# The down products of an expert's second token tile move to the gate and up banks of PSUM

## What is computed

```python
def expert_block(args):
    xb, e = args
    hdn = jax.nn.silu(xb @ w_gate[e]) * (xb @ w_up[e])
    return hdn @ w_down[e]
...
y = y_buf[dest] * gate_sorted[:, None].astype(x.dtype)
return jnp.zeros_like(xf).at[tok_sorted].add(y).reshape(b, s, d)
```

## Time and profile before

| what | value |
|---|---|
| median of 3 runs | 1715.93 us (1715.03 to 1716.71) |
| the profiled execution | 1715.41 us |
| its span, first to last instruction | 1713.2 us |
| its mean granted TensorE clock | 0.973 of full speed |
| TensorE matmuls busy | 1615.4 us, 94% |
| VectorE busy | 1086.8 us, 63% |
| ScalarE busy | 659.3 us, 38% |
| start of expert 1, start of expert 15 | 1053.77 us, 1641.83 us |
| from one expert's start to the next, experts 2 to 15 | 41.63 to 41.68 us |

### The profile page before, as it was taken

How to read it: one execution, slowest core, us unless ns; L and a number is a source line. 1 busy time by engine, 2 the same in 40 slices (tenths; PEclk the granted TensorE clock), 3 DMA queues, 4 the chain that set the end, 5 groups by cost and what they waited for, 6 DMA issues and landing times. The chain is left out here.

```text
span 1713.2 us, 25162 instructions
## 1 busy us (share of the span) xinstructions
PE 1615.4 (94%) x9494; PEld 1398.8 (82%) x9494; DVE 1086.8 (63%) x1799; ACT 659.3 (38%) x919; POOL 340.6 (20%) x271
## 2 busy tenths in 40 slices
PE   6999999999999999999999289999999999999993
PEld 4888888888888888888887178999999999999982
DVE  3436867557676468665586756555676667666676
ACT  2324424143332343342432324344555445544540
POOL 1100005100052001250000012222332323232332
PEclk8999999999999999999999679999999999999997
DMA  7332245332434225352223626666777777777761
GB/s 232 127 99 74 100 146 198 99 98 87 160 139 158 74 75 186 108 182 92 80 93 123 258 84 200 190 203 204 235 250 249 228 238 251 252 228 239 249 182 56
DMA packets 118922, 279.46 MB, mean 163 GB/s; under 512 B 14689, under 2 KB 16865, under 8 KB 118289
## 3 DMA queue, kind: packets, MB, share of 16 engines
q1 hardware_dynamic: 92112, 190.78, 32.8%
q0 software_dynamic: 26112, 84.95, 16.8%
q10 hardware_dynamic: 576, 2.10, 0.3%
HBM read 232.80 MB, written 48.40 MB: 164 GB/s over the span
## 5 line engine op out<-in xcount | busy, mean ns | idle before, releaser
L1054 PE MATMUL mix_acc<-mix_xT_high,mix_w_high 128*128 128x512 f32 x640 | 256.4, 401 | 7.5 <-DVE mix_w_low L791 7.5
L791 DVE TENSOR_TENSOR mix_w_low<-mix_w_raw,mix_w_high 128x2048 fp32r<-128x2048 f32 x73 | 168.5, 2309 | 144.7 <-ACT mix_w_high L646 144.4
L1056 PE MATMUL mix_acc<-mix_xT_high,mix_w_low 128*128 128x512 f32 x640 | 250.9, 392 | 0.0
L1055 PE MATMUL mix_acc<-mix_xT_low,mix_w_high 128*128 128x512 f32 x640 | 250.1, 391 | 0.0
L646 ACT ACTIVATE mix_w_high<-mix_w_raw 128x2048 fp32r<-128x2048 f32 x73 | 139.8, 1915 | 243.4 <-PE mix_acc L1056 224.2
L1789 DVE TENSOR_TENSOR moe_gate_up_low<-kept_w_gate_up_raw,moe_gate_up_high 128x2048 fp32r<-128x2048 f32 x64 | 146.6, 2291 | 80.3 <-ACT moe_gate_up_high L1661 80.3
L2117 PE MATMUL moe_gate_psum<-moe_xT_high,moe_gate_up_high 128*128 128x288 f32 x512 | 154.2, 301 | 1.4 <-DVE moe_xT_low L1806 1.4
L2119 PE MATMUL moe_up_psum<-moe_xT_high,moe_gate_up_low 128*128 128x288 f32 x512 | 152.1, 297 | 0.0
L2118 PE MATMUL moe_gate_psum<-moe_xT_low,moe_gate_up_high 128*128 128x288 f32 x512 | 151.9, 297 | 0.0
L2118 PE MATMUL moe_up_psum<-moe_xT_low,moe_gate_up_high 128*128 128x288 f32 x512 | 151.8, 296 | 0.0
L2117 PE MATMUL moe_up_psum<-moe_xT_high,moe_gate_up_high 128*128 128x288 f32 x512 | 151.6, 296 | 0.0
(11 more groups left out here) (441 smaller groups left out, 3493.2 us busy)
## 6 DMA issues: line engine op xcount, KB each, us to landing
mix_w_raw<-in_w_in SPq DMA_DIRECT2D x57, 1024.0 KB, 5.3
kept_w_gate_up_raw<-in_w_gate SPq DMA_DIRECT2D x32, 1024.0 KB
kept_w_gate_up_raw<-in_w_up SPq DMA_DIRECT2D x32, 1024.0 KB
kept_w_down_raw<-in_w_down SPq DMA_DIRECT2D x32, 1024.0 KB, 10.1
mix_w_raw<-in_w_out SPq DMA_DIRECT2D x16, 1024.0 KB, 5.0
mix_x_rows<-in_x POOLq DMA_DIRECT2D x16, 512.0 KB, 4.5
kept_conv_or_residual<-in_x POOLq DMA_DIRECT2D x16, 512.0 KB, 5.8
x<-kept_conv_or_residual POOLq DMA_DIRECT2D x12, 512.0 KB, 3.3
```

Source lines behind the costliest of these rows:

```text
L791: dve.tensor_tensor(wl[:, stage % 2], raw[:, stage % 2], wh[:, stage % 2].bitcast(F32), ALU.subtract).then_inc(split_l, 1)
L1054: pe.matmul(out, ah, bh, start=first, stop=False)
L1055: pe.matmul(out, ah, bl, start=False, stop=False)
L1056: return pe.matmul(out, al, bh, start=False, stop=last)
```

## The change

The down products of tile B go to `pg[1]` and `pu[1]`, the banks of the gate and up products of chunks 1 and 3. All that reads them there is redirected. The wait of `down` for B on the copies of A is gone, in expert 15 too the wait on A's sum. `down` for A now waits for the copies of the previous expert's A alone. `gate_up` for chunk 1, the next writer of bank 1, waits for the copies of the previous expert's B.

```diff
--- before.py
+++ after.py
@@ -1466,6 +1466,8 @@
         pg = [ps(f"gate_psum{k}", [P, BANK]) for k in range(2)]
         pu = [ps(f"up_psum{k}", [P, BANK]) for k in range(2)]
         py = [ps(f"y_psum{k}", [P, BANK]) for k in range(2)]
+
+        pb = (pg[1], pu[1])
         px = [ps(f"xT_psum{k}", [P, BANK]) for k in range(2)]
 
         xT_at = (px, (pg[0], pu[0]), px[0:1])
@@ -1698,7 +1700,7 @@
                 act.wait_ge((a_used, b_used)[k], r * NE + e + 1)
                 if e:
                     act.wait_ge(added, r * (LAST * COLS * 16) + e * (COLS * 16))
-                act.activation(Y[:, k, 0:BANK], py[0][:], ACT.Copy,
+                act.activation(Y[:, k, 0:BANK], (py, pb)[k][0][:], ACT.Copy,
                                scale=gate[:, COLS * e + k:COLS * e + k + 1]).then_inc(y_act, 1)
 
             def y_quarters(r, e):
@@ -1822,7 +1824,7 @@
                 dve.wait_ge((a_used, b_used)[k], r * NE + e + 1)
                 if e:
                     dve.wait_ge(added, r * (LAST * COLS * 16) + e * (COLS * 16))
-                dve.tensor_scalar(Y[:, k, BANK:], py[1][:], gate[:, COLS * e + k:COLS * e + k + 1], None, ALU.mult)\
+                dve.tensor_scalar(Y[:, k, BANK:], (py, pb)[k][1][:], gate[:, COLS * e + k:COLS * e + k + 1], None, ALU.mult)\
                    .then_inc(y_dve, 1)
 
             def one_hots(r):
@@ -2016,7 +2018,7 @@
                     parts = ((rows, px[1][:, 0:DQ], last[:, 1, LAST:]),)
                 else:
                     c = COLS * LAST + k
-                    parts = [(rows[:, q * BANK:(q + 1) * BANK], py[q][:], gate[:, c:c + 1]) for q in range(2)]
+                    parts = [(rows[:, q * BANK:(q + 1) * BANK], (py, pb)[k][q][:], gate[:, c:c + 1]) for q in range(2)]
                 for part, ps_part, scale in parts:
                     ins = dve.scalar_tensor_tensor(out=part, in0=ps_part, scalar=scale, in1=part,
                                                    op0=ALU.mult, op1=ALU.add)
@@ -2145,6 +2147,9 @@
                 elif n >= 2:
                     pe.wait_ge(hid_done, r * (NE * FC) + n - 1)
                 pe.wait_ge(gu_l, r * (NE * FC) + n + 1)
+                if f == 1 and e:
+                    for done in (y_act, y_dve):
+                        pe.wait_ge(done, r * (2 * LAST) + 2 * e)
                 for c in range(KC):
                     for k, out in enumerate((pg, pu)):
                         ins = three(out[f % 2][:, 0:CAP], wh[:, n % RING, c, k], wl[:, n % RING, c, k],
@@ -2152,15 +2157,9 @@
                 ins.then_inc(gu_used, 1)
 
             def down(r, e, k):
-                if k == B:
-                    if e < LAST:
-                        for done in (y_act, y_dve):
-                            pe.wait_ge(done, r * (2 * LAST) + 2 * e + 1)
-                    else:
-                        pe.wait_ge(end_sum, r * COLS + 2)
-                elif e:
+                if k == A and e:
                     for done in (y_act, y_dve):
-                        pe.wait_ge(done, r * (2 * LAST) + 2 * e)
+                        pe.wait_ge(done, r * (2 * LAST) + 2 * e - 1)
                 for c in range(FC):
                     if k == A:
                         pe.wait_ge(hl_done, r * (NE * FC) + e * FC + c + 1)
@@ -2168,7 +2167,7 @@
                             pe.wait_ge(dn_l, r * (NE * 2) + 2 * e + c // 2 + 1)
                     for q in range(2):
                         s = slice(q * BANK, (q + 1) * BANK)
-                        ins = three(py[q][:], hTh[:, c, AT[k]], hTl[:, c, AT[k]], dh[:, c, s], dl[:, c, s],
+                        ins = three((py, pb)[k][q][:], hTh[:, c, AT[k]], hTl[:, c, AT[k]], dh[:, c, s], dl[:, c, s],
                                     c == 0, c == FC - 1)
                 ins.then_inc((a_used, b_used)[k], 1)
 
```

## The result

The changed kernel takes 1708.25 us (median of 5 runs, 1705.51 to 1708.33), the kernel before beside it 1716.71 us (5 runs, 1715.03 to 1717.55). The ratio is 0.9948, 95% interval 0.9933 to 0.9962: 0.5% faster. On a second chip it was 1707.91 against 1714.57 us, ratio 0.9959 (0.9945 to 0.9972). The profiled span fell from 1713.2 to 1706.5 us, by 6.7 us.

A forecast was written before the change was run, and what follows sets the result against it. TensorE, busy 94% of the span, was taken as the bound. Fifteen handovers at 0.48 us gave 7.2 us, all else 0: execution 1715.41 to 1708.2 us, median 0.5 us above, 1708.7 us; range 1705.5 to 1712.5 us.

The forecast's parts named there:

- The handover, 15 x 0.48 us: Experts 0 to 14, small transposes to B: B's first matmul starts 0.07 us ahead of their end, 0.48 us gained each, 7.2 us.
- the two bounds (0.65 and 0.09 us): Gain per handover: at most 0.65 us with overlap as between equal shapes, at least 0.09 us with fixed 0.41 us load idle.
- The cover of what follows: After B: next expert's weights stay ready ahead, lead 3.4 to 2.9 us; new wait at chunk 1 has 5.6 us of cover.
- Reads beside writes at nothing: ScalarE and VectorE read y banks while TensorE writes gate and up bank 1: no slowdown, priced at nothing.
- Expert 15 at nothing: Last expert: the 3.69 us wait before B goes, but VectorE's chain sets the end, so 0 us gained.
- The half-speed matmuls: Expert 15's B, after its wait: matmuls of 0.63 us against 0.39 may vanish with the wait, also hidden.
- full overlap: Rival at the handover: B's load runs ahead as between equal shapes, 15 x 0.65 = 9.75 us gained, 1706.2 us; chance 0.07.
- The shape taking the wait's place: Rival at the handover: array drain and reload cost about the wait, only 1.4 us gained, 1714.6 us; chance 0.11 (shared).
- The falling clock: Rival in each expert: down products round four banks drop TensorE's clock, fifteen drops cost 25.5 us, 1734.2 us; chance 0.05.

## Why the prediction was right

Forecast 1708.7 us, measured 1708.25 us; a gain of 7.2 us was forecast, 6.7 us measured on the spans and 8.5 and 6.7 us on the medians of two chips. That the two totals lie only 0.45 us apart is partly luck: single executions of the changed kernel went from 1705.51 to 1709.25 us. What shows the forecast's mechanism right is the distance between experts.

- **The handover, 15 x 0.48 us.** Right. B's first matmul starts 0.08 us ahead of the transposes' end; 0.07 was taken. The distance between experts fell by 0.46 to 0.47 us and not by 0.48: B's first two matmuls are 0.34 us apart now and were 0.31 us apart before. The forecast stood on the choice between the two bounds (0.65 and 0.09 us), and the two other changes of shape, from which it was read, gave it rightly.
- **The wait and not the banks.** Shown: with the new banks and the wait kept the ratio is 0.9999, and with the old banks TensorE stands idle for the copies no longer once something covers them.
- **The cover of what follows.** Right: the weights' lead fell from 3.4 to 2.9 us (2.4 us at the start of expert 11), and 5.6 us were forecast and found for the new wait. That this is cover and no accident of the place is shown by the run with the wait at chunk 0, priced from the trace at 4.9 us and measured at 4.94.
- **Reads beside writes at nothing.** Right; the distances of 0.23 us beside the copies show it.
- **Expert 15 at nothing.** Right, and shown apart: 71.33 us from its start to the end with the wait, 71.34 without. The half-speed matmuls vanished in the first profile of the changed kernel (5.40 us for B); in the second B took 6.40 us, hidden as well.
- The rival **full overlap** fell: B starts 0.08 and not 0.24 us ahead. **The shape taking the wait's place** fell: B starts ahead of the transposes' end, and its load shows no idle time at all, since the transposes' loads end only at 1626.98 + 0.56 = 1627.54. The 0.41 us, where it shows, lies beside a matmul in flight. **The falling clock** fell: the granted clock is 1.00 from 1095 to 1635 us.
- The matmul behind every change of shape read here starts 0.06 to 0.08 us ahead of its predecessor's end, against 0.16 us (B to the next gate product above) and 0.24 us (the transposes to A) without a change. The rule of the Trainium skill, TensorEngine Tiling (Array Packing), section Key Properties, that a change of tiling mode drains TensorE, agrees with this. No run here showed what the Trainium skill, TensorE: Matmul & The Clock Gate, section A second HAM failure mode, describes of cycling through PSUM banks.

Not forecast: the start of the experts moved by itself by 0.58 us the wrong way between the two profiles, which is why 7.25 us from expert 0's start on became 6.7 us of span. In expert 0 itself 0.70 us went where 0.46 us is the handover's; the rest is less than what this distance differs by between the two profiles of the changed kernel (44.11 and 44.37 us). Why the medians fell by 8.5 us on one chip and by 6.7 us on the other is not settled beyond this: parts of the time that the change does not touch differ by 1 to 2 us from one profile to the next (expert 0 started between 1008.96 and 1011.21 us, expert 1 took 1.56 us more or less).

## What to carry to other kernels

Before giving a wait more buffers, read what stands between its two sides and how long the next engine's copy takes; here independent work, reordered into the gap, hid the same wait with no bank moved, and saved a change of tile shape besides. Price a removed wait from the moment at which the waiting instruction could start without it, not from the idle time in the row, and look for that moment at a like pair of neighbours. When a wait is moved, ask which instruction already waited for stands behind its releaser in program order: such a wait is free.

## What the hardware showed beyond that

One change of shape fewer was worth 0.22 us per expert, 0.09 us ahead of it and 0.11 us behind it. The idle time of the weight load is no measure of that price: it shows as 0.35 or 0.41 us at most changes, and not at all behind the small transposes, where the matmul starts just as close to its predecessor's end (0.08 us). The same program met a stretch at half clock after the list matmuls in one profile and not in the next (granted 0.83 and 1.00 from 1070 to 1080), which made expert 1 46.26 or 44.70 us long: 1.56 us that no edit explains. With such stretches in a kernel, a gain of a few us is read better from the distances between like stages, here equal within 0.01 us for 13 experts of the changed kernel, than from spans. One pair of equal spans here (1706.5 us) even came about by two such differences that cancel.
